# GpSimd's power operation for the inverse root of the variance, in place of ScalarE's Sqrt and VectorE's RECIPROCAL

## What is computed

```python
def layer_norm(x, g, b):
    mu = mean(x, axis=-1)
    var = mean(square(x - mu), axis=-1)
    return (x - mu) * rsqrt(var + LN_EPS) * g + b

x = layer_norm(ALPHA * x + mixer(x), ln1_g[i], ln1_b[i])
x = layer_norm(ALPHA * x + squared_relu_mlp(x), ln2_g[i], ln2_b[i])
```

## Time and profile before

| | |
|---|---|
| median of 3 runs | 1062.01 us (1061.81 to 1064.13) |
| the profiled execution, its span | 1061.3 us |
| instructions | 21612 |
| TensorE busy | 1045.2 us, 98% |
| VectorE busy | 840.5 us, 79% |
| ScalarE busy | 662.7 us, 62% |
| GpSimd busy | 226.3 us, 21% |

### The profile page before, as it was taken

The page is one execution under the profiler, slowest core; times in us unless marked ns, Lnnn a source line. Parts: engine busy times, 40 slices in busy tenths (PEclk is TensorE's granted clock), DMA queues, the critical chain, the costliest instruction groups (busy, mean ns, idle before and its releaser), DMA issues.

```text
span 1061.3 us, 21612 instructions
## 1 busy us (share of the span) xinstructions
PE 1045.2 (98%) x8247; PEld 1022.6 (96%) x8247; DVE 840.5 (79%) x1289; ACT 662.7 (62%) x1159; POOL 226.3 (21%) x285
## 2 busy tenths in 40 slices
PE   8999999999999999999999999999999999999996
PEld 8999999999999999999999878999999999999995
DVE  6999898989779697696974674888879697696885
ACT  5999858665736547463666775675836647457432
POOL 2111032011111111103234564210111111111023
PEclk9999999999999999999999999999999999999998
DMA  7323214468877877865141211164777877878402
GB/s 255 120 90 100 79 61 141 99 158 159 177 164 158 196 159 157 200 163 197 32 128 46 62 62 40 40 179 81 159 167 163 194 156 155 201 159 177 136 11 75
DMA packets 54460, 139.54 MB, mean 131 GB/s; under 512 B 5632, under 2 KB 21440, under 8 KB 54368
## 3 DMA queue, kind: packets, MB, share of 16 engines
q0 software_dynamic: 14512, 53.60, 29.7%
q1 hardware_dynamic: 39584, 84.32, 24.3%
q10 hardware_dynamic: 288, 0.59, 0.2%
HBM read 135.95 MB, written 3.56 MB: 131 GB/s over the span
## 4 chain that ended last, share of the span: by engine, by line
PE 92%; DVE 2%; ACT 2%; issue 1%; POOL 1%; DMA 1%; SPq 0%; DVEq 0%; POOLq 0%; ACTq 0%
PE bank L2493 8%; PE bank L2474 8%; PE bank L2495 8%; PE bank L2219 8%; PE bank L2494 8%; PE bank L2475 8%; PE bank L2476 8%; PE bank L2220 8%; PE bank L2221 8%; PE bank L2306 3%; PE bank L2307 3%; PE bank L2308 3%; PE bank L2614 1%; PE bank L2588 1%; PE bank L2447 1%
## 5 line engine op out<-in xcount | busy, mean ns | idle before, releaser
L832 ACT ACTIVATE w_hi<-stage 128x1024 fp32r<-128x1024 f32 x164 | 168.3, 1053 | 128.9 <-DMA stage<-w_up 74.1
L1352 DVE TENSOR_TENSOR w_lo<-stage,w_hi 128x1024 fp32r<-128x1024 f32 x164 | 197.0, 1219 | 57.8 <-ACT w_hi L832 57.7
L2493 PE MATMUL bank<-part_hi,w_hi 128*128 128x288 f32 (+1 forms) x672 | 195.5, 291 | 0.0
L2495 PE MATMUL bank<-part_hi,w_lo 128*128 128x288 f32 (+1 forms) x672 | 194.9, 290 | 0.0
L2494 PE MATMUL bank<-part_lo,w_hi 128*128 128x288 f32 (+1 forms) x672 | 194.3, 289 | 0.0
L2219 PE MATMUL bank<-x_hi,w_hi 128*128 128x288 f32 (+1 forms) x496 | 145.2, 293 | 1.0 <-issue 1.0
L2220 PE MATMUL bank<-x_lo,w_hi 128*128 128x288 f32 (+1 forms) x496 | 143.7, 290 | 0.0
L2221 PE MATMUL bank<-x_hi,w_lo 128*128 128x288 f32 (+1 forms) x496 | 143.1, 288 | 0.0
L2493 PEld LDWEIGHTS bank<-part_hi,w_hi 128*128 128x128 f32 x672 | 127.2, 189 | 1.8 <-issue 1.8
L2494 PEld LDWEIGHTS bank<-part_lo,w_hi 128*128 128x128 f32 x672 | 127.5, 190 | 0.0
L2495 PEld LDWEIGHTS bank<-part_hi,w_lo 128*128 128x128 f32 x672 | 127.3, 189 | 0.0
(11 more groups left out here) (295 smaller groups left out, 2913.4 us busy)
## 6 DMA issues: line engine op xcount, KB each, us to landing
stage<-w_up SPq DMA_DIRECT2D x54, 512.0 KB, 3.7
stage<-w_down SPq DMA_DIRECT2D x52, 512.0 KB, 4.2
stage<-w_down POOLq DMA_DIRECT2D x48, 512.0 KB, 5.6
stage<-w_up POOLq DMA_DIRECT2D x44, 512.0 KB, 5.7
stage<-w_qkv SPq DMA_DIRECT2D x10, 512.0 KB, 4.1
stage<-w_x SPq DMA_DIRECT2D x8, 512.0 KB, 5.4
stage<-w_y SPq DMA_DIRECT2D x8, 512.0 KB, 3.5
stage<-w_out SPq DMA_DIRECT2D x8, 512.0 KB, 3.7
```

The source lines that it names most:

```text
L832: A(w_hi[:, slot_of(l, k), :], raw_of(l, c, k), ACT.Copy).then_inc(s_whi, 1)
L1352: vt.tensor_tensor(w_lo[:, s, :], raw_of(l, c, k), w_hi[:, s, :].bitcast(F32), ALU.subtract)\
L2493: mm(out, wh, xh[:, k, :], start=(fresh and k == 0), stop=False, skip_group_check=True)
L2495: ins = mm(out, wl, xh[:, k, :], start=False, stop=(k == 1), skip_group_check=True)
```

## The change

Seven times ScalarE's Sqrt and VectorE's RECIPROCAL are replaced by one TENSOR_TENSOR with the operation power on GpSimd: `msq`, with an exponent tile of -0.5 that is broadcast along the columns. The exponent is set once at the start. In the last pass the same is done on three columns. The new instruction stands in GpSimd's queue right behind the sums of squares of its half, waits for the variance, and before it overwrites `rstd` for the reader of the pass before.

```diff
@@ ScalarE, norm_stats
                 A(mean[:, :n], unit(m0)[:, :n], ACT.Copy).then_inc(s_evA, 1)
-                act.wait_ge(s_var, idx + 1)
-                A(rstd[:, :n], msq[:, :n], ACT.Sqrt).then_inc(s_std, 1)
@@ ScalarE, at the end
             A(fin[:, 0:3], bank[0:96, column_bank, 0:3], ACT.Square).then_inc(s_finsq, 1)
-            act.wait_ge(s_finvar, 1)
-            A(fin[:, 4:7], fin[:, 4:7], ACT.Sqrt).then_inc(s_finstd, 1)
@@ VectorE, norm_apply
                 dve.wait_ge(s_std, idx + 1)
-                ordered(vt.reciprocal(rstd[:, :n], rstd[:, :n]))
+                dve.wait_ge(s_seqV, seq[0])
@@ VectorE, at the end
             dve.wait_ge(s_finstd, 1)
-            ordered(vt.reciprocal(fin[:, 8:11], fin[:, 4:7]))
@@ GpSimd, at the start
+            exponent = dv[:, 5, :]
+            pt.memset(exponent[:, 0:1], -0.5).then_inc(s_seqP, 1)
             pool.wait_ge(s_vec, 16)
+            pool.wait_ge(s_seqP, 1)
@@ GpSimd
+            def inverse_root(L, h):
+
+                _, n = HALF[h]
+                idx = 2 * L + h
+                pool.wait_ge(s_var, idx + 1)
+                if idx:
+                    pool.wait_ge(s_xhat, 4 * idx)
+                pt.tensor_tensor(rstd[:, :n], msq[:, :n], exponent[:, 0:1].broadcast_to([128, n]), ALU.pow).then_inc(s_std, 1)
@@ GpSimd, tiles
                     add_square(L, pos // KT, pos % KT)
+                    if pos % KT == KT - 1:
+                        inverse_root(L, pos // KT)
@@ GpSimd, mlp
                 for m in range(KT):
                     add_square(L, 0, m)
+                inverse_root(L, 0)
                 if l:
                     residual(L, 0)
                 for m in range(KT - l):
                     add_square(L, 1, m)
                 if l:
+                    pool.wait_ge(s_finvar, 1)
+                    pt.tensor_tensor(fin[:, 8:11], fin[:, 4:7], exponent[0:96, 0:1].broadcast_to([96, 3]), ALU.pow).then_inc(s_finstd, 1)
...
+                inverse_root(L, 1)
                 residual(L, 0)
                 residual(L, 1)
@@ GpSimd, before the second tiles
             add_square(2, 0, late_now(16))
+            inverse_root(2, 0)
             tiles(2)
```

More of the change, by code:

```diff
@@ L249, in build @@
         s_redhi, s_redlo, s_ones = sem("sum_hi_done"), sem("sum_lo_done"), sem("ones_rounded")
-        s_var, s_std = sem("variance_ready"), sem("deviation_ready")
+        s_var, s_std = sem("variance_ready"), sem("inverse_root_ready")
         s_xhat, s_y, s_ylo, s_res = sem("normed"), sem("y_ready"), sem("y_lo_done"), sem("residual_done")
@@ L279, in build @@
         s_fin, s_finsq, s_finvar = sem("final_sums_done"), sem("final_mean_squared"), sem("final_variance_ready")
-        s_finstd, s_diag, s_finroot = sem("final_deviation_ready"), sem("diagonal_ready"), sem("final_root_spread")
+        s_finstd, s_diag, s_finroot = sem("final_inverse_root_ready"), sem("diagonal_ready"), sem("final_root_spread")
         s_yfin = sem("y_out_vector")
```

## The result

The change takes 1320.66 us (median of 5 runs, 1320.58 to 1322.99) against 1062.01 before (5 runs, 1061.81 to 1064.13). The ratio is 1.2434 with a 95% interval of 1.2421 to 1.2447: 258.7 us slower. The prediction was slower, 1077, with a range to 1120: the direction was right and the size was wrong, by a factor of seventeen in the loss.

The account below looks back on a forecast made before the run. TensorE, 98% busy, was taken as the bound. To the profiled 1061.3 us it added 11.4 of LayerNorm delays, 0.3 at the end and 3.4 of half clock: 1076.4, with 0.7 for the median 1077; range 1060.9 to 1120.

Parts of the forecast that it names:

- What bounds the kernel: TensorE, busy 98% of the span; its waits at the interior LayerNorms leave about half a microsecond to gain.
- The price of the power: GpSimd's power instruction, priced as two iterated functions and two simple steps: 8.1 us at 256 columns, 9.1 at 288.
- P: Time of one GpSimd power instruction at 256 columns; 1.125 times that at 288 columns.
- The chain of dependent steps: Inside the power on GpSimd: 4 cycles for each dependent step, an estimated 34 us for 256 columns.
- The estimate by section 3.1: Inside the power on GpSimd: about 3 operations per cycle, 40 steps in 2.8 us, making the change free.
- Cover and room: At each LayerNorm, TensorE's delay is the power's time less the old reciprocal's cover and spare time; 11.4 us in sum.
- LN0: First of eight LayerNorms, numbered idx = 2L + h; delay 3.9 us, at TensorE's sums for the next LayerNorm.
- The queue: GpSimd's additions of squares and accumulating weight DMAs standing behind the waiting power; costed at nothing.
- LN7: Narrow last LayerNorm, three columns, on the path to the end: +0.3 us.
- The half clock: TensorE's clock at 0.50 after long waits, 1.7 us lost per stretch; one behind LayerNorms 0 and 2 each, 3.4 us.
- The very long power: Rival: each step of GpSimd's power waits for the one before, 12 to 19 us; 1127 us at 15; chance 0.13.
- The short power: Rival: steps overlap inside GpSimd's power, about 2.0 us, nothing waits below 4.0; time 1061.6, not slower; chance 0.40.

Follow-up runs that it names:

- The short instruction: Changed kernel with GpSimd's power in the first seven LayerNorms replaced by a one-input minimum instruction at the same place: 1062.27 us beside 1062.18 for before, ratio 0.9999.
- The price list: Kernel before, with eleven GpSimd instructions timed singly behind its last work, powers of several widths, exponents and partitions, multiplication and addition: 41.16 us for 256 columns of power.
- LN1 and LN5 alone: Kernel before with the power for all 288 columns of these two LayerNorms only, Sqrt and RECIPROCAL kept elsewhere: 1132.11 us, ratio 1.0647.
- 60 columns within the cover: Kernel before with the power for the first 60 of 288 columns of LayerNorms 1 and 5, Sqrt and RECIPROCAL otherwise: 1063.16 us beside 1063.84, ratio 0.9996.
- 44 columns: Changed kernel with 44 columns of each LayerNorm through the power and the rest through a short minimum instruction: 1083.72 us, ratio 1.0199.
- the queue alone: Kernel before, Sqrt and RECIPROCAL kept, with GpSimd also running unread powers of as many columns behind each variance: 1261.27 us (one run).

## Why the prediction was wrong, by its steps

**What bounds the kernel: right.** TensorE's waits were the place to look, and the old waits held so little that nothing could be gained. The short instruction, with an unchanged time, shows it.

**The price of the power: the step that failed.** "In GpSimd's 784 ns this is 2 x 4.2 x 0.784 + 2 x 0.784 = 8.1 us, and 9.1 at 288 columns." Measured 41.5 and 46.7. The ratio 4.2 is how VectorE's iteration stands to its own simple operation and said nothing of GpSimd's power. Worse, the upper bound was no bound: 40 steps at 0.48 us are 19 us, and the instruction costs 2.2 times that, 160 ns a column. I had counted the steps and priced each as a pass that streams over all columns. The stated range (to P near 14) fell with it.

The chain of dependent steps that I set beside it, an estimated 34 us by the Trainium skill's page "GPSIMD Engine Reference", section 7, was nearest to the measured 41.5. The price list shows a fixed cost for each column that neither data nor lanes change, which such a chain would have; it doesn't show the chain. Why the power takes 160 ns a column stays open. The estimate by section 3.1 of the same page of the Trainium skill, 2.8 us, is contradicted for this operation.

**Cover and room: right within a tenth.** With the measured P the prediction's own terms give, against the waits in the trace:

| | terms with 41.5 and 46.7 us | measured TensorE wait |
|---|---|---|
| LN0 | 37.3 | 32.9, and about 2 at the sums |
| LN1 | 34.3 | 32.2 |
| LN2 | 36.6 | 32.7, and 1.3 more |
| LN3 | 39.5 | 39.3 |
| LN4 | 35.1 | 30.4, and about 2 at the sums |
| LN5 | 34.3 | 31.1 |
| LN6 | 34.1 | 32.9 |
| sum | 251.2 | 237.5 |

With 0.3 and seven times 1.7 of half clock they come to 1325 us; the median is 1320.7. Two runs check the terms on their own: LN1 and LN5 alone, 64.7 us for 68.6, and 60 columns within the cover at nothing. Why the list is some 5% too high I haven't tested.

At LN0 and LN4 the path was another one than the prediction's. It looked for TensorE's wait at the sums of the next half. Nearly all of it stands a few us earlier in TensorE's order, at the first product of the half just normalised, and 2 us are left at the sums. The product before, and in the change:

```profile
169.69 0.28 PE L2306 MATMUL bank<-x_hi,w_hi 128*128 128x256 f32 x1
...
203.43 0.58 PE L2320 MATMUL bank<-x_hi,w_hi 128*128 128x256 f32 x1 [32.94 <-DVE w_lo L1342]
```

With 44 columns, a delay of 5 us by the list, TensorE waits 3.2 us at the sums, as the prediction has it, and 0.8 at the product; with the whole power the order is turned round.

**The queue: cheap only where the power is short.** "I cost it at nothing" holds for 10 us, and the prediction's remark on the squares ("they are made from tiles that VectorE adds after the same wait") is why the two causes lie side by side. But at 41 us the queue alone costs 199 us, where the whole change costs 259. The prediction has that only as a remark on LN1, that without the cover the held DMAs "would be a wait of the same length as the slip"; ScalarE standing behind its two square buffers at LN0 (42.5 us) it doesn't have.

**LN7:** +0.5 us, for +0.3; a power of three columns takes 0.86.

**The half clock:** 17.9 us of added busy time over seven stalls is 2.6 each, for 1.7 counted. The prediction took each stretch to be as long as the one at the start, 3.41 us. Behind LN0 and LN1 that nearly holds (3.7 and 3.6). Behind the other five the clock stayed at 0.50 for 4.4 to 8.2 us after the wait, and at LN4 it went down once more for 3.4. The recorded figures for a very long power also count five stretches where all seven delays are longer than 2.1 us; with seven, the 1127 would be 1130. In the kernel with 44 columns the granted clock went down three times between the LayerNorms, behind LN2, LN3 and LN4, where LN0 and LN2 had been counted.

**The rivals.** The very long power came nearest, with a chance of 0.13, and ended at 19 us. Nothing in the rows spoke for it but the count of steps, and its reason, that each step waits for the one before, no run shows. The short power, to which I gave 0.40, is what the first experiment put in its place.

## What to carry to other kernels

An operation that no row shows has no upper bound in the rows of simple operations: here it costs 67 times a multiplication of the same shape on the same engine. Measure it once, alone, at two widths, before it goes into a queue. An engine at 21% is not idle capacity for one long instruction: list what is queued behind it and how many buffers its users have, because that can cost nearly as much as the wait for the result. And if the bound engine waits for half a microsecond in all, half a microsecond is all that a faster side path can bring.

## What the runs showed of the hardware

- GpSimd's power of fp32 tiles costs 160 ns a column and about 0.3 us fixed: 41.16 us for 256 columns, 20.72 for 128, 10.5 for 64. At 64 columns it is the same for 1, 8, 17 and 128 partitions and for exponents -0.5, -1.37 and 0; at 256 columns for 16 and 128 partitions, for exponents -0.5, 1 and 2, and for a broadcast or a full exponent tile. A multiplication of 128x256 takes 0.61 us.
- Three powers in a row, without a wait between them, take 31.5 us, three times one.
- GpSimd's one-input instruction with a minimum and a multiplication took 1.44 us for 256 columns, where its multiplication by a scalar takes 0.48.
- TensorE's granted clock was at 0.50 in the last 29.9 us of a 32.9 us wait, and stayed there for 3.7 us after it had work again; behind the six other long waits it was 3.6 to 8.2 us.
